# Which engine makes the low parts of the mixers' weights, in a kernel of two transformer blocks

## What is computed

```
for layer in range(DEPTH):                                   # DEPTH = 2
    shift_m, scale_m, gate_m, shift_f, scale_f, gate_f = adaln_modulation(c, *ada[layer])
    h = rmsnorm(x, pre_m) * (1.0 + scale_m) + shift_m
    x = x + gate_m * rmsnorm(mixers[layer](h), post_m)
    h = rmsnorm(x, pre_f) * (1.0 + scale_f) + shift_f
    x = x + gate_f * rmsnorm(swiglu(h, *ffns[layer]), post_f)
```

```
    proj = h @ w_in[l]
    merged = sigmoid(gate_a) * (moba_attention(q, k, v) @ moba_w_proj[l]) \
           + sigmoid(gate_b) * (gmlp_spatial_gating(gu, gv, ...) @ gmlp_w_proj[l])
    x = x + merged @ w_out[l]
    x = x + memory_cross_attention(h, m, ...)
    x = x + peer_ffn(h, peer_w_q[l], peer_subkeys[l], peer_w_down[l], peer_w_up[l])
return rmsnorm_2(x, final_g)
```

## Time and profile before

| | |
|---|---|
| median of 3 runs | 2167.47 us (2166.73 to 2170.33) |
| the profiled execution | 2166.55 us |
| its span, first to last instruction | 2164.4 us |
| granted TensorE clock, mean | 0.954 of full speed |
| matmuls, busy | 1961.8 us (91%) |
| VectorE, ScalarE, GpSimd, busy | 1384.9, 979.8, 653.3 us |

### The profile page before, as it was taken

The page is one execution under the profiler, slowest core; times in us unless marked ns, Lnnn a source line. Parts: engine busy times, 40 slices in busy tenths (PEclk is TensorE's granted clock), DMA queues, the critical chain, the costliest instruction groups (busy, mean ns, idle before and its releaser), DMA issues.

```text
span 2164.4 us, 33504 instructions
## 1 busy us (share of the span) xinstructions
PE 1961.8 (91%) x13340; PEld 1807.4 (84%) x13340; DVE 1384.9 (64%) x2380; ACT 979.8 (45%) x1415; POOL 653.3 (30%) x285
## 2 busy tenths in 40 slices
PE   6778889995969778999989889899999999999998
PEld 5776689995967657998888789899998888999997
DVE  5787765546892677333733334998887888666665
ACT  5334454444433334444544544556664333444444
POOL 2451534444641423433865646500000000000000
PEclk9889989997989889999999999999999999999999
DMA  7552456663545324554543334457776676565443
GB/s 294 187 171 92 147 185 235 248 227 110 185 145 214 118 78 155 189 184 173 180 138 136 122 112 156 139 183 220 211 215 239 252 256 243 204 234 195 184 179 124
DMA packets 94234, 392.82 MB, mean 181 GB/s; under 512 B 7648, under 2 KB 41584, under 8 KB 55552
## 3 DMA queue, kind: packets, MB, share of 16 engines
q1 hardware_dynamic: 94080, 390.69, 51.3%
HBM read 372.83 MB, written 15.73 MB: 180 GB/s over the span
## 4 chain that ended last, share of the span: by engine, by line
PE 69%; DVE 16%; ACT 3%; POOL 3%; issue 2%; DMA 0%; DVEq 0%; ACTq 0%; SPq 0%; POOLq 0%
PE ps L559 9%; PE ps L561 9%; PE ps L560 9%; PE acc L555 8%; PE acc L556 7%; PE acc L557 7%; DVE arena L1290 3%; POOL wlo L1261 3%; PE acc L559 2%; PE acc L560 2%; PE acc L561 2%; DVE arena L1441 2%; DVE arena L1763 2%; PE acc L1216 1%; PE ps L1216 1%
## 5 line engine op out<-in xcount | busy, mean ns | idle before, releaser
L2236 ACT ACTIVATE whi<-raw 128x1024 fp32r<-128x1024 f32 x559 | 589.7, 1059 | 543.5 <-PE acc L557 273.5
L1261 POOL TENSOR_TENSOR wlo<-raw,whi 128x1024 fp32r<-128x1024 f32 x247 | 621.0, 2526 | 687.0 <-ACT whi L2236 686.1
L559 PE MATMUL ps<-hhi,whi 128*128 128x256 f32 x1880 | 545.0, 290 | 31.0 <-POOL wlo L1261 13.6
L560 PE MATMUL ps<-hlo,whi 128*128 128x256 f32 x1880 | 539.2, 287 | 0.0
L561 PE MATMUL ps<-hhi,wlo 128*128 128x256 f32 x1880 | 539.0, 287 | 0.0
L1261 DVE TENSOR_TENSOR wlo<-raw,whi 128x1024 fp32r<-128x1024 f32 x312 | 389.5, 1249 | 230.9 <-ACT whi L2236 230.9
L559 PEld LDWEIGHTS ps<-hhi,whi 128*128 128x128 f32 x1880 | 368.6, 196 | 37.7 <-issue 16.4
L560 PEld LDWEIGHTS ps<-hlo,whi 128*128 128x128 f32 x1880 | 368.5, 196 | 2.9
L561 PEld LDWEIGHTS ps<-hhi,wlo 128*128 128x128 f32 x1880 | 367.9, 196 | 0.0
L555 PE MATMUL acc<-whi,chi 128*128 128x512 f32 x752 | 296.7, 395 | 4.6 <-POOL wlo L1261 3.0
L556 PE MATMUL acc<-whi,clo 128*128 128x512 f32 x752 | 295.3, 393 | 0.0
(11 more groups left out here) (448 smaller groups left out, 2567.5 us busy)
## 6 DMA issues: line engine op xcount, KB each, us to landing
raw<-in_peer_down SPq DMA_DIRECT2D x64, 1024.0 KB, 5.0
raw<-in_peer_up SPq DMA_DIRECT2D x64, 1024.0 KB, 5.3
arena<-in_ada SPq DMA_DIRECT2D x80, 512.0 KB, 4.2
raw<-in_w_gate SPq DMA_DIRECT2D x22, 1024.0 KB, 4.8
raw<-in_w_up SPq DMA_DIRECT2D x22, 1024.0 KB, 4.9
raw<-in_w_down SPq DMA_DIRECT2D x22, 1024.0 KB, 4.8
arena<-spill SPq DMA_DIRECT2D x14, 1024.0 KB, 7.1
spill<-hT_t SPq DMA_DIRECT2D x22, 448.0 KB, 6.2
```

The costliest lines, as they stand in the source:

```text
L559: e.matmul(out, hi, xh, start=start, stop=False, skip_group_check=True)
L560: e.matmul(out, hi, xl, start=False, stop=False, skip_group_check=True)
L1261: e.tensor_tensor(out=lo, in0=w, in1=hi.bitcast(F32), op=ALU.subtract).then_inc(*X(("lo", j)))
L2236: e.activation(hi, w, ACT.Copy, scale=1.0).then_inc(*self.A(("hi", j)))
```

## The change

`lo_engine` gives 114 of GpSimd's 247 blocks to VectorE: all of the mixers' but nine at their heads (FIRST), and but the projections gmlp_proj, moba_proj and w_out2. By stage: 23 in the projection and SSD of layer 0, 12 in MLA's output, 30 in the projection and GLA of layer 1, 16 in NSA, 33 in the second block's mixer. GpSimd keeps 133. TensorE also waits once for GpSimd's second `xd`, which before was made ahead of cuts that it waited for.

```
+FIRST = (("w_low", 0, 0), ("w_low", 0, 1), ("w_low", 1, 0), ("w_glr", 0, 0), ("w_gqk", 0, 0), ("w_gqk", 0, 1),
+         ("w_mqk", 0, 0), ("w_mqk", 0, 1), ("w_mqk", 1, 0))
@@ lo_engine @@
         if name[:6] in ("w_gate", "w_up0", "w_up1", "w_down"):
             return ("V", "G")[j % 2]
-        return "V" if name[:5] == "peer_" and j >= self.block_no["peer_down", VLO0 // 2, VLO0 % 2] else "G"
+        if name[:5] == "peer_":
+            return "V" if j >= self.block_no["peer_down", VLO0 // 2, VLO0 % 2] else "G"
+        if name in ("gmlp_proj", "moba_proj", "w_out2", "xa_k", "xa_v", "xa_q", "xa_o"):
+            return "G"
+        return "G" if (name, i, half) in FIRST else "V"
@@ pe_ssd @@
         for i in range(0, 8, 2):
+            if i == 0:
+                e.wait_ge(*self.at("xd", 1))
             if i % 4 == 0:
                 e.wait_ge(*self.at("mixed", i // 4))
```

## The result

The changed kernel takes 2109.91 us (median of 4 runs, 2106.82 to 2112.52), the one before 2167.1; the ratio is 0.9734, with a 95% interval of 0.9716 to 0.9752.

The account below looks back on a forecast made before the run. TensorE, its matmuls busy 91% of the span, was taken as the bound, with time to win only in its idles or lower clock. Terms -22 + 2.5 - 21 - 5.5 + 8 = -38 us gave 2130 us, range 2110 to 2160.

Parts of the forecast that it names:

- The mechanism: VectorE instructions on SBUF operands wait until GpSimd's cut ends; relief about 1.6 and 2.1 us per cut taken at 1.25.
- The signs of all five parts: Layer 0 -22 us, MLA +2.5, layer 1's projection and GLA -21, NSA -5.5, second block's mixer +8.
- the two large ones: Layer 0's projection and SSD, forecast -22 us; layer 1's projection and GLA, forecast -21 us.
- MLA's +2.5: MLA's output projection: two cuts late behind softmax and ada, 2 x 1.25 us, between 0 and 5.
- The two idles of the second mixer: TensorE waits for cuts behind the rotary steps: 3.8 us at `w_mqk` 3, 3.4 at `w_gu`.
- L1912 at 1.22: Rotary step in the second block's mixer, formerly L1904: 1.22 us each without GpSimd's stalls, against 2.8 before.
- the clock's term in the sum: Second block's mixer: two blocks at the lower clock behind new idles, 2.4 us more a block, +5 us.
- more than the sum: Rival, chance 0.08: granted clock also rises in layer 0's and layer 1's stretches, 17 us more, 2113.
- In SSD: Layer 0's SSD, where VectorE is full: 14.9 us of stalls less 8 cuts, 10.0, saves 5.
- In the convolution: Layer 0: each later round falls from 8.96 us to some 7.5; three and a half rounds give 5.
- Only VectorE's own balance counts: Rival, chance 0.22: time is won only where VectorE is full; layer 0 -8 us, in all -18, 2150.
- VectorE becomes the bound: Rival, chance 0.08, slower: stalls not given back, VectorE's added work pushes TensorE, 2245; decided by relief under 1.25 us a cut.

Follow-up runs that it names:

- layer 0 alone: Only the 23 cuts of layer 0's projection and SSD moved to VectorE, from the kernel before: 2140.09 us, ratio 0.9876.
- The second mixer alone: Only the 33 cuts of the second block's mixer moved to VectorE, from the kernel before: 2172.06 us, ratio 1.0025.

## Why the prediction was wrong

**What held.** The mechanism: an instruction of VectorE on SBUF operands waits for GpSimd's. Every slow row that the prediction used is fast in the changed kernel, and the kernel with unneeded subtractions on GpSimd makes those of layer 0's projection slow again. (With GpSimd only writing, instructions with two SBUF inputs are not held: it is its reads that count for them.) The signs of all five parts were right, and the idle of the two large ones to 3 us: 22 forecast and 19.3 measured, 21 and 20.2. MLA's +2.5 was +2.4, which is luck: it was a middle between 0 and 5 that no row showed, and idle rose by 3.0. The two idles of the second mixer were put at 3.8 and 3.4 us and are 3.67 both; L1912 at 1.22 is 1.24.

**The step that failed is the clock's term in the sum.** The prediction charged it once, as a cost: "two such blocks behind the new idles are 5". It gave nothing for the old idles that go, though its own terms take 48.5 us of idle out of three parts. The same rows would have said so: 0.85 and 0.89 of granted clock in the two stretches, where the idle was. Measured, matmul time fell by 18.9 us, a third of the gain. With the idle terms as forecast (-43 in all) and this one, the sum would have been -62; the idle itself came to -36. The two errors, 24 us and 7, have opposite signs.

It stood among the rivals, as "more than the sum", priced at 17 us for 2113, and was given a chance of 0.08; its 17 is close to the 18.9 measured. It was no rival at all but part of the main case: a term that is charged for an idle made has to be credited for an idle removed. The price of one such idle was high too. It was taken as 2.4 us, from a block that ran wholly at 0.50; most cost about 1.5 (3.04 to 4.52 behind an idle of 2.96). Where it was charged, in `w_mqk` and `w_gu`, matmul time rose by 4.3 us (35.90 to 40.21) for the 5 forecast, but that agreement is luck: 2.4 of it is in the stretch behind the two new idles (18.14 to 20.55), and 1.9 (17.76 to 19.66) in the one before, behind a third wait that the prediction didn't have. Over the whole of that mixer it fell by 2.0, since from `w_gab` 1 on, behind the old idle of 4.71 us, it went from 94.1 to 88.9.

**Smaller misses.** Idle in the second mixer rose by 5.3, not 3. This third wait is one that I had overlooked: VectorE's program waits for the table of sines ahead of the stage's first three cuts, which before stood on GpSimd. It idles 6.98 us at 987.15 for that load (above), and TensorE then waits 1.78 us for the cut of `w_mqk` 1.1. The load was not moved in any run, so what this is worth is open. In SSD I let VectorE's own balance set the end and took 5; TensorE's idle in the linears `w_z` 0 and 1 went to nothing, and with the clock they became 8.4 us shorter. In the convolution the round became 7.03 and not 7.5.

**The other rivals.** "Only VectorE's own balance counts" (2150) falls: layer 0 alone gave 27.6 us, where it had 8. "VectorE becomes the bound" falls too: VectorE is 28.5 us less busy than before with 135.9 us more of cuts, a relief of 1.44 us a cut over the whole kernel against the 1.25 that decide. The second mixer alone, though, is that rival in small: its 33 cuts brought a relief of about 1.0 us each (VectorE went from 88.31 to 96.06 us in this part), under 1.25, and the kernel with these alone is 4.4 us slower.

## What to carry to other kernels

Work moved from GpSimd to VectorE can leave VectorE less busy, if its instructions with SBUF operands were waiting for GpSimd's: compare the same instruction's duration beside a busy and an idle GpSimd before pricing either. Price TensorE's idle in both directions: here the idles of 2.96 us and more that were looked at cost about 1.4 to 2.4 us of slower matmuls on top, and 36 us of idle removed took 18.9 us of matmul time with them. And where an engine takes on work that another did in parallel, look for its longest unbroken sequence ahead of that work and put the work inside it.

## What the runs showed that I had not expected

- A GpSimd that only writes holds a tensor-by-constants instruction (0.410 to 0.756 us) but none with two SBUF inputs (0.752 and 1.221 unchanged).
- GpSimd is held by VectorE as well: its 128x1024 subtraction took 2.935 us in the mean beside a busy VectorE, and 2.41 in the experts' part.
- In the experts' part the price of an idle in slower matmuls was the same, 1.4 to 1.5 us, for idles of 2.96, 5.45 and 7.86 us, and nothing for 1.89. In the mixers one of 4.71 cost 2.4, and of two short ones at the same place the one of 1.78 us cost 1.5 and the one of 1.69 nothing.
- The same program's executions differ by up to 11 us (2124.62 to 2136.08), with a mean granted clock of 0.964 and 0.957.
